# Order of two weight requests in the loop over experts: the present expert's down weights ahead of the next expert's gate and up rows

## The chip, the cores and the metric

The kernel runs on one core of one Trainium2 chip. The metric is the device time of one execution in microseconds (us). Engines are named as in the profile: PE is the matrix engine and PEld its weight loads, DVE the vector engine, ACT the scalar engine, POOL the general engine that issues gathers and scatters, and SP the engine whose instruction queue issues nearly all other DMAs (its rows are called SPq). One MB in the text is 1024 KB.

## The reference, cut to what matters

One encoder layer over 1024 tokens of width 1024: a token mixing half (projections, a convolution branch, chunked attention, merge, LayerNorm), and then a mixture of 16 experts, which is the part that the change touches.

```python
def grouped_moe(h, w_router, b_router, w_gate_up, w_down):
    ...
    combine = jnp.einsum("tk,tke->te", weights,
                         jax.nn.one_hot(sel_idx, N_EXPERTS, dtype=jnp.float32)).astype(t.dtype)
    out = jnp.zeros_like(t)
    for e in range(N_EXPERTS):
        g, u = jnp.split(t @ w_gate_up[e], 2, axis=-1)
        out = out + combine[:, e:e + 1] * ((jax.nn.silu(g) * u) @ w_down[e])
    return out.reshape(b, s, d)
```

Each token goes to two experts (TOP_K = 2), and each expert has a gate and up matrix of 1024x1024 and a down matrix of 512x1024, in float32.

## The kernel before, in words

**Tiles.** The router's result is sorted on the chip into tiles of up to 128 (token, expert) rows, each with one expert. With this input there are 21 tiles for 16 experts (`total`, line 1241): the lines of the mixture show 21 tiles, of which experts 3, 7, 8, 9 and 10 have two each and the other eleven have one. Tile 0 is expert 0's, tiles 3 and 4 are expert 3's, tile 5 expert 4's, tiles 8 to 15 are those of experts 7 to 10, tile 16 expert 11's and tile 20 expert 15's. A table `tab` says for each tile its expert (T_E), and whether the step of this tile splits the gate and up rows of the next expert (T_SPLIT_GU, set where tile i is the first of its expert) or the down rows (T_SPLIT_DN, set where tile i-1 was the first of its expert).

**Weights and their halves.** A float32 product is made of three matmuls (`mm3`, lines 1223 to 1226) of a high and a low part. So every weight row that lands is split: ACT copies the high part, DVE subtracts it and keeps the low part. For the gate and up rows these are `gu_high` (L1140) and `gu_low` (L1146), for the down rows `down_rows` on ACT (L1332) and on DVE (L1510). DVE counts `dn_lo` up by one for each of the FC = 4 down chunks that it has split.

**Buffers.** `gu` has two places, one for even and one for odd experts, each with 8 row blocks of raw (and low) and high part. `dn_raw` is single, as are `dn_h` and `dn_l`. Expert e+1's gate and up rows can land only where expert e-1's were, so `load_gu` waits for each pair of row blocks until PE has used it in the last tile of expert e-1 (`gu_rows`, L1101). Expert e's down weights can land only once `dn_raw` has been split for expert e-1 (`dn_lo`, L1121).

**Queue.** Both kinds of request are issued in order on SP in `sync_part`. Expert e+1's gate and up rows are four requests of 1 MB (L1102), expert e's down weights one request of 2 MB (L1105). Ahead of the loop SP has issued the gate and up rows of experts 0 and 1 and the down weights of expert 0. SP issues nothing else in the loop; POOL issues the gather of the tile's rows (L1161) and the scatter of its results (L1171).

**A step.** Each engine runs a step for each tile i, in its own fixed order:

- PE: transpose the gathered rows of tile i (L1248); down product of tile i-2 (`down`, 24 matmuls); transpose h of tile i-1 (L1269); gate and up product of tile i (`up`, 48 matmuls).
- ACT: high part of the transposed rows (`x_t`, L1324); if due, high parts of the down rows of tile i-1's expert (L1332), which first wait for `dn_in` and for the down product of tile i-2; high part of h of tile i-1 (L1338); if due, high parts of the next expert's gate and up rows (L1140), which wait for `gu_in` pair by pair; silu of tile i (L1348), which waits for PE's `up(i)`.
- DVE: low parts in the same order (L1504, L1510, then `y` of tile i-2, L1531, then L1514, L1146), then the product of gate and up (L1522).

So for an expert e whose first tile is i, step i splits expert e+1's gate and up rows, and step i+1 splits expert e's down rows.

Of the kernel before, what the change touches and what calls it, by code (L numbers as in the profile page):

```python
# [30 lines left out]
FC = FF // P  # L31
# [984 lines left out]
def moe(nc, sem, m):  # L1016
# [78 lines left out]
    def load_gu(sp, e, rows_before=None, pairs=range(4)):  # L1095

        for j in pairs:
            if e:
                sp.wait_ge(gu_in[j], 16 * e)
            if rows_before is not None:  # L1100
                sp.wait_ge(gu_rows, rows_before + (j + 1))  # L1101
            sp.dma_start(gu[:, place_of(e), 2 * j:2 * j + 2, 1, :].bitcast(F32), wexp[e][:, 2 * j:2 * j + 2, :]).then_inc(gu_in[j], 16)  # L1102

    def load_dn(sp, e):
        sp.dma_start(dn_raw[:], wexp[e][:, KC:WROWS, :]).then_inc(dn_in, 16)  # L1105

    def sync_part(sp):
        sp.wait_ge(x1_out, 16 * TT)
        sp.wait_ge(acc_out, 16 * TT)
        sp.wait_ge(xt_r, TT)  # L1110
        load_gu(sp, 1)
        sp.wait_ge(lg_done, TT)
        load_dn(sp, 0)
        sp.wait_ge(ids_done, 2)
        sp.wait_ge(tables, 1)
        for e in range(1, NE):
            if e + 1 < NE:

                load_gu(sp, e + 1,
                        sp.value_load(rows_i[0:1, e - 1:e], min_val=0, max_val=4 * MAX_TILES - 4))  # L1120
            sp.wait_ge(dn_lo, FC * e)  # L1121
            load_dn(sp, e)
        total = sp.value_load(cum_i[0:1, NE - 1:NE], min_val=NE, max_val=MAX_TILES)
        sp.wait_ge(gu_rows, 4 * total)
        sp.dma_start(g2_b[:], ln2_g.partition_broadcast(P)).then_inc(ln2_in, 16)
        sp.dma_start(b2_b[:], ln2_b.partition_broadcast(P)).then_inc(ln2_in, 16)
        sp.wait_ge(y_out, total * 16)
        for t in range(TT):
            sp.dma_start(xf[:, t, :], acc_dram[P * t:P * t + P, :]).then_inc(row_in[t], 16)
        for t in range(TT):  # L1130
            sp.wait_ge(f_ok, t + 1)
            sp.dma_start(out[P * t:P * t + P, :], xf[:, t, :]).then_inc(f_out, 16)
        sp.wait_ge(f_out, 16 * TT)
# [242 lines left out]
    def vector_part(dve):  # L1376
# [200 lines left out]
        for t in range(TT + 2):  # L1577
# [10 lines left out]
    return {"load_expert_0": lambda sp, j0, j1: load_gu(sp, 0, pairs=range(j0, j1)),  # L1588
            "gate_up_high_0": lambda act, k0, k1: gu_high(act, 0, place_of(0), range(k0, k1)),
            "gate_up_low_0": lambda dve, k0, k1: gu_low(dve, 0, place_of(0), range(k0, k1)), "sync": sync_part, "gpsimd": pool_part, "tensor": tensor_part,  # L1590
            "transpose_x1": transpose_x1, "logits": logits, "scalar": scalar_part, "copy_x1t": copy_x1t,
            "vector": vector_part}
# [41 lines left out]
```

## Time and profile before

| what | us |
|---|---|
| median of 3 runs | 1306.51 |
| lowest and highest run | 1303.16 and 1320.21 |
| the profiled execution's own time | 1301.75 |
| its span, first to last instruction | 1299.9 |
| PE busy (share of the span) | 1139.8 (88%) |
| DVE busy | 831.9 (64%) |
| ACT busy | 518.9 (40%) |

The mixture's tiles run from 845 to about 1250 us of the span; the loop over experts on SP issues from 854.9 to 1214.1 us. A row's start is from the start of the span. In a timeline row the first number is the start, the second the length of the merged group, and the bracket the idle time of the engine ahead of it with what ended it.

### The profile page before, as it was taken

Reading aid. Unit: us, or ns where it says so; the run is one execution under the profiler, and the core shown is the slowest. Engines: PE = TensorE matmul, PEld = TensorE weight load, DVE = VectorE, ACT = ScalarE, POOL = GpSimd, SP = SyncE. Lnnn points to the kernel's source line nnn. Section 1 sums busy time; section 2 is a strip of 40 time slices with the busy share of each in tenths; the row PEclk is TensorE's granted clock in tenths of the full one; section 3 lists DMA queues with packets and bytes.
Section 4 is the critical chain, followed back from the end, with each engine's and each line's share of the span. In section 5 each row is a group of like instructions: output and inputs, shape, how many; then the busy total and the mean of one; then the engine's idle time right before and its main releaser. Section 6 shows DMA issues by size and latency. Waiting matters only on the chain.

```text
span 1299.9 us, 17045 instructions
## 1 busy us (share of the span) xinstructions
PE 1139.8 (88%) x5600; PEld 947.6 (73%) x5601; DVE 831.9 (64%) x1128; ACT 518.9 (40%) x732; POOL 113.5 (9%) x105
## 2 busy tenths in 40 slices
PE   7999999997989999799799997289999999999720
PEld 6888888776777787677688786267888888887610
DVE  4899899215364626555476555879689655689436
ACT  5111111233375636544333212147468433467212
POOL 0000000000000000000000000002222122122118
PEclk9999999998999999899899997589999999999865
DMA  6122333320001001330513235269889876689543
GB/s 231 49 89 65 97 97 98 98 81 33 33 17 40 32 20 49 139 153 33 196 49 146 96 131 199 118 228 359 298 318 401 270 245 224 216 328 397 171 130 161
DMA packets 47701, 199.45 MB, mean 153 GB/s; under 512 B 5152, under 2 KB 5408, under 8 KB 45600
## 3 DMA queue, kind: packets, MB, share of 16 engines
q1 hardware_dynamic: 41456, 176.19, 36.1%
q0 software_dynamic: 6192, 22.55, 6.9%
q8 instruction: 34, 0.56, 0.2%
q14 instruction: 19, 0.16, 0.0%
HBM read 166.21 MB, written 32.51 MB: 153 GB/s over the span
## 4 chain that ended last, share of the span: by engine, by line
PE 73%; DVE 9%; ACT 7%; issue 5%; DMA 2%; POOL 2%; ACTq 1%; DVEq 1%; POOLq 0%; SPq 0%
PE ps L411 16%; PE ps L413 15%; PE ps L412 15%; PE ps L1224 7%; PE ps L1226 7%; PE ps L1225 7%; ACT gu L1140 2%; PE ps L1220 1%; POOL xf L1204 1%; PE ps L1248 1%; ACT pth L729 1%; DVE ptl L903 1%; DVE gu L1146 1%; PE ps L497 1%; POOL xf L1200 1%
## 5 line engine op out<-in xcount | busy, mean ns | idle before, releaser
L411 PE MATMUL ps<-xh,wh 128*128 128x512 f32 x512 | 205.9, 402 | 10.0 <-DVE xl L793 8.1
L412 PE MATMUL ps<-xl,wh 128*128 128x512 f32 x512 | 202.3, 395 | 0.0
L413 PE MATMUL ps<-xh,wl 128*128 128x512 f32 x512 | 202.1, 395 | 0.0
L816 DVE SCALAR_TENSOR_TENSOR cv<-u,dw_t,cv 128x1024 f32<-128x1024 f32 x120 | 154.1, 1284 | 3.7
L1146 DVE TENSOR_TENSOR gu<-gu (+1 forms) x128 | 147.0, 1217 | 9.1 <-ACT gu L1140 9.0
L1140 ACT ACTIVATE gu<-gu (+1 forms) x128 | 124.4, 1048 | 50.2 <-DMA gu<-in_wexp 42.4
L1224 PE MATMUL ps<-gu,xgh 128*128 x336 | 134.0, 399 | 9.0 <-DVE xgl L1504 9.0
L1226 PE MATMUL ps<-gu,xgl 128*128 x336 | 131.9, 392 | 0.0
L1225 PE MATMUL ps<-gu,xgh 128*128 x336 | 131.8, 392 | 0.0
L411 PEld LDWEIGHTS ps<-xh,wh 128*128 128x128 f32 x512 | 97.7, 191 | 33.3 <-issue 12.2
L788 DVE TENSOR_TENSOR wl<-raw,wh 128x1024 fp32r<-128x1024 f32 x52 | 63.5, 1223 | 83.8 <-ACT wh L635 83.6
L413 PEld LDWEIGHTS ps<-xh,wl 128*128 128x128 f32 x512 | 97.8, 191 | 21.2
L412 PEld LDWEIGHTS ps<-xl,wh 128*128 128x128 f32 x512 | 97.9, 191 | 20.2 <-issue 0.5
L1510 DVE TENSOR_TENSOR dn_l<-dn_raw,dn_h 128x1024 fp32r<-128x1024 f32 x64 | 74.1, 1219 | 43.3 <-ACT dn_h L1332 43.3
L1158 POOL COPY id_now<-ids_i 128x1 int32 (+1 forms) x22 | 15.0, 682 | 949.2 <-DVE to_i L1497 836.3
L635 ACT ACTIVATE wh<-raw 128x1024 fp32r<-128x1024 f32 x52 | 54.4, 1054 | 93.9 <-DMA raw<-in_wblk 93.9
L1332 ACT ACTIVATE dn_h<-dn_raw 128x1024 fp32r<-128x1024 f32 x64 | 62.4, 1047 | 73.3 <-PE ps L1226 73.3
L1224 PEld LDWEIGHTS ps<-gu,xgh 128*128 128x128 f32 x336 | 63.6, 189 | 23.5 <-issue 10.8
L1224 PE MATMUL ps<-dn_h,hbh 128*128 128x512 f32 x168 | 69.4, 413 | 12.0 <-DVE hbl L1514 7.4
L1226 PEld LDWEIGHTS ps<-gu,xgl 128*128 128x128 f32 x336 | 63.6, 189 | 13.6
L1225 PEld LDWEIGHTS ps<-gu,xgh 128*128 128x128 f32 x336 | 63.7, 190 | 12.8
L1225 PE MATMUL ps<-dn_l,hbh 128*128 128x512 f32 x168 | 67.6, 402 | 0.0
(217 smaller groups left out, 2133.9 us busy)
## 6 DMA issues: line engine op xcount, KB each, us to landing
gu<-in_wexp SPq DMA_DIRECT2D x64, 1024.0 KB
dn_raw<-in_wexp SPq DMA_DIRECT2D x16, 2048.0 KB
raw<-in_wblk SPq DMA_DIRECT2D x52, 512.0 KB, 3.6
gate_cols<-gst SPq DMA_DIRECT2D x16, 512.0 KB, 5.0
xraw<-in_xT SPq DMA_DIRECT2D x8, 512.0 KB, 7.8
gcm<-gate_cols SPq DMA_DIRECT2D x8, 512.0 KB, 7.9
gam<-gate_cols SPq DMA_DIRECT2D x8, 512.0 KB, 15.1
x<-in_x SPq DMA_DIRECT2D x8, 512.0 KB, 6.6
```

The source lines that it names most:

```text
L411: pe.matmul(o, a_h, b_h, start=first, stop=False)
L412: pe.matmul(o, a_h, b_l, start=False, stop=False)
L413: return pe.matmul(o, a_l, b_h, start=False, stop=last)
L788: dve.tensor_tensor(lo, src, hi, ALU.subtract).then_inc(w_lo, 1)
L816: dve.scalar_tensor_tensor(out=cv[:, j, :], in0=tap, scalar=w, in1=cv[:, j, :], op0=ALU.mult, op1=ALU.add).then_inc(conv_d, 1)
L1140: eng.activation(gu[:, par, k, 0, :], gu[:, par, k, 1, :].bitcast(F32), ACT.Copy).then_inc(gu_hi, 1)
L1146: eng.tensor_tensor(gu[:, par, k, 1, :], gu[:, par, k, 1, :].bitcast(F32), gu[:, par, k, 0, :], ALU.subtract).then_inc(gu_lo, 1)
L1224: pe.matmul(o, a_h, b_h, start=first, stop=False)
L1225: pe.matmul(o, a_h, b_l, start=False, stop=False)
L1226: return pe.matmul(o, a_l, b_h, start=False, stop=last)
L1332: act.activation(dn_h[:, k, :], dn_raw[:, k, :], ACT.Copy).then_inc(dn_hi, 1)
L1510: dve.tensor_tensor(dn_l[:, k, :], dn_raw[:, k, :], dn_h[:, k, :], ALU.subtract).then_inc(dn_lo, 1)
```

## The change

In the loop the wait for `dn_lo` and the request of the down weights of expert e come first, and the four requests of expert e+1 with their waits follow. The number of requests, their sizes and every wait are as before; only their order in SP's program changes.

```diff
         for e in range(1, NE):
+            sp.wait_ge(dn_lo, FC * e)
+            load_dn(sp, e)
             if e + 1 < NE:
 
                 load_gu(sp, e + 1,
                         sp.value_load(rows_i[0:1, e - 1:e], min_val=0, max_val=4 * MAX_TILES - 4))
-            sp.wait_ge(dn_lo, FC * e)
-            load_dn(sp, e)
```

## Rows read from the trace of the kernel before

**Rows 1.** The page: span, and the chain that ended last by engine

```profile
span 1299.9 us, 17045 instructions
...
PE 73%; DVE 9%; ACT 7%; issue 5%; DMA 2%; POOL 2%; ACTq 1%; DVEq 1%; POOLq 0%; SPq 0%
```

**Rows 2.** Windows: us, busy time of PE, PEld, DVE, ACT, POOL; granted clock, DMA share, GB/s

```profile
870.80:926.70 55.90, 54.78 (x260) 45.37 (x259) 50.62 (x48) 39.14 (x44) 12.73 (x11) 1.00 0.87 316
1016.60:1159.60 143.00, 143.00 (x679) 118.78 (x678) 84.46 (x81) 65.09 (x74) 26.08 (x32) 1.00 0.77 264
```

**Rows 3.** Timeline of SP's queue: requests of the expert weights

```profile
803.40 2.13 SPq L1102 DMA_DIRECT2D gu<-in_wexp  x4
...
870.83 0.34 SPq L1105 DMA_DIRECT2D dn_raw<-in_wexp  x1
871.86 6.23 SPq L1102 DMA_DIRECT2D gu<-in_wexp  x4
889.91 0.34 SPq L1105 DMA_DIRECT2D dn_raw<-in_wexp  x1
...
924.10 8.53 SPq L1102 DMA_DIRECT2D gu<-in_wexp  x4
932.68 0.49 SPq L1105 DMA_DIRECT2D dn_raw<-in_wexp  x1
941.84 8.53 SPq L1102 DMA_DIRECT2D gu<-in_wexp  x4
962.18 0.34 SPq L1105 DMA_DIRECT2D dn_raw<-in_wexp  x1
```

**Rows 4.** Timeline of DVE: the splits of the down rows (L1510)

```profile
866.18 4.62 DVE L1510 TENSOR_TENSOR dn_l<-dn_raw,dn_h 128x1024 fp32r<-128x1024 f32 x4
...
922.05 4.63 DVE L1510 TENSOR_TENSOR dn_l<-dn_raw,dn_h 128x1024 fp32r<-128x1024 f32 x4 [1.88 <-ACT dn_h L1332]
...
957.52 4.63 DVE L1510 TENSOR_TENSOR dn_l<-dn_raw,dn_h 128x1024 fp32r<-128x1024 f32 x4 [4.09 <-ACT dn_h L1332]
...
1011.96 4.63 DVE L1510 TENSOR_TENSOR dn_l<-dn_raw,dn_h 128x1024 fp32r<-128x1024 f32 x4 [0.55 <-ACT dn_h L1332]
...
1154.98 4.63 DVE L1510 TENSOR_TENSOR dn_l<-dn_raw,dn_h 128x1024 fp32r<-128x1024 f32 x4 [4.09 <-ACT dn_h L1332]
...
1209.45 4.63 DVE L1510 TENSOR_TENSOR dn_l<-dn_raw,dn_h 128x1024 fp32r<-128x1024 f32 x4 [0.50 <-ACT dn_h L1332]
```

**Rows 5.** Timeline of ACT: splits of gate and up rows, and two silus

```profile
912.65 2.01 ACT L1140 ACTIVATE gu<-gu  x2 [0.54 <-DMA gu<-in_wexp]
...
932.27 0.60 ACT L1348 ACTIVATE hb<-ps 128x512 f32<-128x512 f32 x1 [6.92 <-PE ps L1226]
...
941.27 7.70 ACT L1140 ACTIVATE gu<-gu  x8 [1.52 <-issue]
...
968.30 0.57 ACT L1348 ACTIVATE hb<-ps 128x512 f32<-128x512 f32 x1
```

**Rows 6.** Timeline of DVE: what follows a split of gate and up rows

```profile
942.52 9.17 DVE L1146 TENSOR_TENSOR gu<-gu  x8 [1.79 <-ACT gu L1140]
951.61 0.68 DVE L1522 TENSOR_TENSOR hb<-hb,ps 128x512 f32<-128x512 f32 x1
952.21 1.22 DVE L1504 TENSOR_TENSOR xgl<-ps,xgh 128x1024 fp32r<-128x1024 f32 x1
```

**Rows 7.** Windows around the burst that SP requests at 803.40 us

```profile
803.40:808.40 5.00, 3.10 (x15) 3.00 (x15) 1.32 (x5) 1.07 (x2) 0.00 (x0) 0.50 0.76 261
808.40:820.00 11.60, 1.22 (x4) 0.93 (x4) 10.57 (x32) 8.01 (x8) 0.00 (x0) 0.50 1.04 429
820.00:822.00 2.00, 0.00 (x0) 0.00 (x0) 1.93 (x3) 0.00 (x0) 0.00 (x0) 0.50 0.02 8
```

**Rows 8.** DMA queues in 860 to 1240 us: POOL's gathers and scatters

```profile
q0 software_dynamic: 5616, 20.45, 21.0%
```

**Rows 9.** Window of the down product of tile 19, after idle time of PE

```profile
1225.40:1233.10 7.70, 7.67 (x25) 6.12 (x25) 0.00 (x0) 0.00 (x0) 0.19 (x1) 0.70 0.21 83
```

**Rows 10.** The page: the group of ACT's down row splits

```profile
L1332 ACT ACTIVATE dn_h<-dn_raw 128x1024 fp32r<-128x1024 f32 x64 | 62.4, 1047 | 73.3 <-PE ps L1226 73.3
```

## The prediction

> **What bounds the kernel now.** I read the page first [rows 1]: 73% of the chain that ended last is PE, DMA 2%, so PE sets the time as a whole. But that is an average. The change lies in SP's loop, so I then read that part in windows [rows 2]. Where experts have two tiles (1016.6 to 1159.6 us) PE is busy without a gap: 143.0 us for 8 tiles, 17.9 us a tile of 72 matmuls and 12 short transposes (so some 0.23 us a matmul), with the DMA engines 77% busy. Where experts have one tile (870.8 to 926.7, four steps), they are 87% busy and PE still 98%. So PE bounds both, and DMA stands right behind it in the second kind. That is the row to worry about: every such step has to bring in 6 MB.
>
> Third view, SP's queue [rows 3], against the DVE timeline [rows 4]. It tells which wait held each request. The down request at 870.83 comes right after the down rows of expert 0 were split (866.18 + 4.62 = 870.80), the one at 889.91 likewise. There `dn_lo` is what SP waits for. At 932.68 it is not: the split had ended at 926.68, and the down request stood 6.0 us behind the four gate and up requests (924.10 to 932.63). This happens for e = 4, 8, 9, 10 and 11, where expert e-1 has two tiles. Is 6 us of use there? ACT's splits of the down rows idled 73.3 us, all of it until a PE matmul [rows 10]. None ended with the landing of the down weights. So an earlier landing buys nothing.
>
> **The change part by part.** Nothing is added or removed; five requests an expert (6 MB) swap places, and the wait for `dn_lo` now stands ahead of all five.
>
> Part 1, e = 4, 8, 9, 10, 11. The down request goes out 6 us sooner, worth 0 by the paragraph above. The first gate and up request waits for `dn_lo`: at e = 4 it goes from 924.10 to about 926.68 plus 1.0 (the distance of 870.83 to 871.86, [rows 3]), 3.6 us later; the last one stays where PE frees its rows. 2 MB are now ahead of them. From the down request to the last pair's landing I count 20.8 us (below), so 926.7 + 20.8 = 947.5. ACT starts on these rows at 941.27 and comes to the last pair 5.8 us later, at 947.0 [rows 5]. Cost 0.5 us on ACT, and DVE, which is slower (9.17 us for 8 against 7.70, [rows 5, 6]), hides it. I take 0; if that cover were gone it would be 0.5 us each, 2.5 in all.
>
> Part 2, e = 1, 2, 3, 5, 6, 7, 12, 13, 14: expert e-1 has one tile. Here lies the cost. Take e = 5. Before, expert 6's gate and up rows are requested from 941.84 on, while PE works through tile 5 [rows 3]. The wait for `dn_lo` ends only at 957.52 + 4.63 = 962.15 [rows 4], in step 6. And step 6 is the one in which ACT and DVE split expert 6's gate and up rows, whose request now starts at 963.2. They were requested 21 us ahead (first pair); now they are requested inside the step that needs them. Nothing hides that: ACT and DVE run in order, so silu and the product of this tile, the copies of the next tile's rows and the next split of down rows all stand behind L1140. And that next split is what SP waits for. It closes a ring:
>
> request → 6 MB land → last two row blocks split → next step's down split → request.
>
> Its length, term by term.
>
> - Request to last landing. The nearest row is the burst at 803.40: 4 MB and 2 MB, nothing else in flight. 261 GB/s for 5.0 us and 429 for 11.6 are 6.28e6 bytes, the whole of the 6 MB, and the engines are idle from 820.0 on [rows 7]. That is 16.7 us. POOL's gather and scatter of the step go through the same DMA engines: 21.0% of 380 us over 39 of them (20 gathers, 19 scatters) is 2.05 us each [rows 8]. The scatter is triggered by L1531, right behind the down split, and the gather by L1248, which PE reaches about 7 us after it, so both fall into the burst: 16.7 + 4.1 = 20.8 us. From below it is 16.7 (neither in it). From above it is 22.75: in the loaded trace, from the down request at 889.91 to the moment when the last pair of that round lets ACT go on, 912.65 [rows 3, 5]. I take 20.8, since in that row earlier requests were still in the queue.
> - Landing to end of the down split. ACT needs 1.0 us a block, DVE starts 1.25 us after ACT (942.52 against 941.27) and takes 1.15 a block: 3.5 us for the last pair. Then L1522 at 0.60 and L1504 at 1.15 pitch, then four blocks of L1510, 4.63 [rows 4, 6]: 9.9 us. ACT's silu (0.57, [rows 5]), its copy of the tile's rows and its own down blocks run beside this. From below 9.0, if DVE keeps up with the first block; from above 10.5.
> - SP's wake up: 870.83 - 870.80, 0.03 us; I take 0.05.
>
> One ring is 0.05 + 20.8 + 9.9 = 30.75 us. PE isn't on it: `up` and `down` are 48 and 24 matmuls, 11.0 and 5.5 us at 0.23 each, and have 30 to fit in.
>
> Nine of these replace what the trace shows from one end of a down split to another [rows 4]: 870.80 to 926.68, 962.15 to 1016.59, 1159.61 to 1214.08, together 164.8 us. Nine rings are 276.75, less 2.05 for the first (no scatter exists before tile 0 is done): 274.7. Difference +109.9 us.
>
> Part 3, leaving a ring. After each of the three runs PE sets the pace again and must first catch up. Before, `up` ended 5.6 us after the down split (932.27 against 926.68, [rows 4, 5]), 6.8 in the other two places. After, `up` starts 5.5 us after the last landing (0.2 past L1504) and needs 11.0, while the down split ends at 9.9: 6.6. Also PE has idled some 12 us in a ring, and after an idle time of 7 us the trace shows a granted clock of 0.70 over a down product, 7.70 us for what takes 5.5 at full clock [rows 9]: 2.2 more, now on the path. 8.8 less 5.6, and less 6.8 twice: 7.2 us in all. Within the rings the slower clock costs nothing, since PE has 14 us to spare there.
>
> Sum: 109.9 + 7.2 = 117 us, on the profiled execution's 1301.75 (span 1299.9): 1419. The median of the runs is 4.8 above that execution; I name 1421, a little toward it.
>
> A page of the Trainium skill speaks of one term. The trace has 6 MB at 429 GB/s in its long window [rows 7]. "DMA: Bandwidth & Descriptors", section "Where 436 GB/s comes from", says that for transfers from HBM to SBUF the HBM side, about 358 GB/s for a core, binds. By that rule the burst would take about 3 us more and nine rings 26 us more, an estimate from the page. The trace doesn't agree with the rule in its one undisturbed burst.
>
> **The rivals.**
>
> A. The transfers are slower than in the lone burst, because gather and scatter cost them more than their own 2.05 us. For it: 22.75 us in the loaded row. Against it: there the queue wasn't empty at the start. Ring 32.7, nine 294.3 (no allowance for the first), +129.5 + 7.2: 1438.
>
> By the estimate from the page, 358 GB/s would come out near A too, at 1445.
>
> B. Gather and scatter fall outside the burst, or POOL's packets cost SP's nothing. Ring 26.65, nine 239.9, +75.1 + 7.2: 1384.
>
> C. PE falls to half clock in each ring and stays there: `up` 20.6, `down` 10.3, transposes some 2 more. The down split of the next ring waits for `down` (L1332's own wait), and the ring becomes some 34.4 us: +144.8 + 16: 1462. Against it: PE would then be busy nearly all of the ring, and what the trace shows after an idle time is a return to full clock within one down product [rows 9].
>
> D. The other side: faster. Place: the requests of e = 4, 8, 9, 10, 11. If the landing of the down weights, and not PE, were the last of the two waits of L1332, five requests sent 6.0 us sooner would give back 30 us. It decides only if the later requests of Part 2 land before ACT comes to them, that is, with over 20 us of slack: 1272. Against it: the row names PE for all 73.3 us [rows 10], and ACT already waited for a gate and up pair at 912.65 with the early requests [rows 5], so there is no slack. If it gave nothing back and cost nothing, the time would stay at 1302 to 1307.
>
> **How the numbers follow.** The forecast's own case (ring 29 to 32) 0.65, A 0.15, B 0.13, C 0.04, D and no change together 0.03. The predicted time is 1421. The range takes in most of A and B: 1388 to 1446. A measurement of this kernel tells about 2% from no change (its three runs lie within 1.3% of each other); all cases but D are slower by 6% or more: faster 0.01, same 0.02, slower 0.97.
>
> **What would show it.** In the profile of the changed kernel: nine times SP issues a down request and four gate and up requests within some 4 us, right after the end of a down split, at a distance of about 31 us; ACT's L1140 waits for the DMA in nine steps, over 9 us each, where the trace of before has waits like the 0.54 at 912.65 [rows 5]; DMA share falls to some 0.65 in these stretches, and PE's clock dips in them. The stretch of experts 7 to 10 keeps 17.9 us a tile. The down splits still wait for PE or for nothing. It would be wrong if L1140's long waits were absent, if the rings were under 26 or over 33 us, or if the two-tile stretch grew.

## The result, and the profile after

The changed kernel takes 1439.4 us in the median of four runs (1436.3 to 1442.7), the kernel before 1304.8 in the same comparison: ratio 1.1005, 95% interval 1.0916 to 1.1094. The forecast was 1421 in a range of 1388 to 1446. Direction and mechanism came out as said. The size was 18 us short: it lies at the value of rival A (1438), and the range holds it because it takes in that rival.

The page of the changed kernel. DMA is now 14% of the chain that ended last, and PE 64%, where [rows 1] have 2% and 73%.

```profile
span 1437.5 us, 17045 instructions
...
PE 64%; DMA 14%; DVE 8%; issue 5%; ACT 4%; POOL 2%; SPq 1%; DVEq 1%; ACTq 0%; POOLq 0%
```

SP's queue in the changed kernel, to be read beside [rows 3].

```profile
906.62 0.34 SPq L1105 DMA_DIRECT2D dn_raw<-in_wexp  x1
907.67 2.24 SPq L1102 DMA_DIRECT2D gu<-in_wexp  x4
939.49 0.34 SPq L1105 DMA_DIRECT2D dn_raw<-in_wexp  x1
...
1146.91 0.34 SPq L1105 DMA_DIRECT2D dn_raw<-in_wexp  x1
1147.94 4.89 SPq L1102 DMA_DIRECT2D gu<-in_wexp  x4
...
1286.32 0.34 SPq L1105 DMA_DIRECT2D dn_raw<-in_wexp  x1
1287.35 2.21 SPq L1102 DMA_DIRECT2D gu<-in_wexp  x4
1318.56 0.34 SPq L1105 DMA_DIRECT2D dn_raw<-in_wexp  x1
1319.58 2.21 SPq L1102 DMA_DIRECT2D gu<-in_wexp  x4
1350.75 0.34 SPq L1105 DMA_DIRECT2D dn_raw<-in_wexp  x1
```

In the one-tile places all four gate and up requests follow the down request within 3.6 us, none of them held by PE any more, and the next group comes some 32.2 us later (1286.32, 1318.56, 1350.75; the second ring of the loop is the longest, 32.9). This is the ring of the prediction. ACT and DVE show its inside, for the ring that starts at 1318.56.

ACT:

```profile
1331.97 2.01 ACT L1140 ACTIVATE gu<-gu  x2 [15.64 <-DMA gu<-in_wexp]
1334.49 2.00 ACT L1140 ACTIVATE gu<-gu  x2 [0.51 <-DMA gu<-in_wexp]
1338.33 2.00 ACT L1140 ACTIVATE gu<-gu  x2 [1.84 <-DMA gu<-in_wexp]
1340.86 2.00 ACT L1140 ACTIVATE gu<-gu  x2 [0.52 <-DMA gu<-in_wexp]
1342.77 0.58 ACT L1348 ACTIVATE hb<-ps 128x512 f32<-128x512 f32 x1
```

DVE:

```profile
1313.90 4.62 DVE L1510 TENSOR_TENSOR dn_l<-dn_raw,dn_h 128x1024 fp32r<-128x1024 f32 x4
...
1342.09 2.36 DVE L1146 TENSOR_TENSOR gu<-gu  x2 [0.17 <-ACT gu L1140]
1344.37 0.68 DVE L1522 TENSOR_TENSOR hb<-hb,ps 128x512 f32<-128x512 f32 x1
1344.97 1.22 DVE L1504 TENSOR_TENSOR xgl<-ps,xgh 128x1024 fp32r<-128x1024 f32 x1
1346.10 4.62 DVE L1510 TENSOR_TENSOR dn_l<-dn_raw,dn_h 128x1024 fp32r<-128x1024 f32 x4
```

ACT's eight blocks were one row without a gap in [rows 5]; now they are four pairs, and ACT sits idle 15.6 us ahead of the first. "Last landing" is here the moment at which ACT, having waited for it, starts on the last pair. From the request (1318.56) to the last landing (1340.86) are 22.3 us, from there to the end of the down split (1350.72) 9.9, and SP issues 0.03 later.

The waits of the changed kernel from 860 to 1380 us (who waited, for whom, us in total, times, longest):

```profile
ACT gu L1140 <- DMA gu<-in_wexp: 177.7, 46, 16.3
DVE gu L1146 <- ACT gu L1140: 148.5, 42, 13.6
...
ACT dn_h L1332 <- PE ps L1226: 26.1, 6, 11.3
```

And its windows, with the columns of [rows 2]:

```profile
876.00:971.70 95.70, 61.57 (x250) 49.02 (x250) 51.38 (x49) 41.04 (x45) 7.33 (x11) 0.79 0.61 225
1010.80:1107.50 96.70, 57.48 (x238) 45.88 (x237) 52.56 (x49) 41.03 (x45) 8.90 (x12) 0.79 0.64 228
1254.10:1350.70 96.60, 58.88 (x242) 46.88 (x241) 52.50 (x49) 41.04 (x45) 8.92 (x12) 0.79 0.63 228
```

The three runs of one-tile experts take 95.7, 96.7 and 96.6 us, where they took 55.9, 54.4 and 54.5 [rows 4]: +124.1 of the 137.6 us by which the spans differ. No engine is busy for more than two thirds of them, DMA neither: each waits for another in turn. The stretches behind the first two of these runs grew by 3.7 and 3.6 us and the end by 1.0. The remaining 5.2 lie ahead of the loop, where the two programs are the same; an experiment with the new order below has its first down split end at 868.6 us, ahead of both, so this isn't the change's.

### The profile page after: what moved, and what is told of

It reads as the page before. It is cut to its first block, busy times and chain, and to the rows that moved or that the text cites. A ratio compares the mean times of both kernels' runs of the same rounds, so it can differ in the third digit from the quotient of the medians.

```text
span 1437.5 us, 17045 instructions
## 1 busy us (share of the span) xinstructions
PE 1171.7 (82%) x5600; PEld 968.1 (67%) x5601; DVE 835.2 (58%) x1128; ACT 520.5 (36%) x732; POOL 96.6 (7%) x105
## 3 DMA queue, kind: packets, MB, share of 16 engines
q1 hardware_dynamic: 41456, 176.19, 32.9%
## 4 chain that ended last, share of the span: by engine, by line
PE 64%; DMA 14%; DVE 8%; issue 5%; ACT 4%; POOL 2%; SPq 1%; DVEq 1%; ACTq 0%; POOLq 0%
PE ps L411 15%; PE ps L413 14%; PE ps L412 14%; DMA gu<-in_wexp 13%; PE ps L1224 6%; PE ps L1225 5%; PE ps L1226 5%; PE ps L1220 1%; POOL xf L1204 1%; DVE dn_l L1510 1%; PE ps L497 1%; ACT pth L729 1%; DVE ptl L903 1%; PE ps L1248 1%; SPq L1102 1%
## 5 line engine op out<-in xcount | busy, mean ns | idle before, releaser
L1146 DVE TENSOR_TENSOR gu<-gu (+1 forms) x128 | 150.2, 1221 | 149.2 <-ACT gu L1140 148.5
L1140 ACT ACTIVATE gu<-gu (+1 forms) x128 | 127.6, 1049 | 224.1 <-DMA gu<-in_wexp 219.5
L1224 PE MATMUL ps<-gu,xgh 128*128 x336 | 142.3, 423 | 11.2 <-DVE xgl L1504 10.1
L1225 PE MATMUL ps<-gu,xgh 128*128 x336 | 138.9, 413 | 0.0
L1226 PE MATMUL ps<-gu,xgl 128*128 x336 | 138.5, 412 | 0.0
L1269 PE MATMUL ps<-ident_t,hb 128*128 128x128 f32 x84 | 17.3, 342 | 105.4 <-DVE hb L1522 105.4
L1224 PEld LDWEIGHTS ps<-gu,xgh 128*128 128x128 f32 x336 | 68.7, 205 | 30.2 <-issue 15.9
L635 ACT ACTIVATE wh<-raw 128x1024 fp32r<-128x1024 f32 x52 | 54.4, 1054 | 94.6 <-DMA raw<-in_wblk 94.6
L1510 DVE TENSOR_TENSOR dn_l<-dn_raw,dn_h 128x1024 fp32r<-128x1024 f32 x64 | 74.0, 1220 | 23.3 <-ACT dn_h L1332 23.3
L1269 PEld LDWEIGHTS ps<-ident_t,hb 128*128 128x128 f32 x84 | 12.3, 173 | 110.9 <-DVE hb L1522 109.5
L1226 PEld LDWEIGHTS ps<-gu,xgl 128*128 128x128 f32 x336 | 67.9, 202 | 15.4
L1225 PEld LDWEIGHTS ps<-gu,xgh 128*128 128x128 f32 x336 | 68.4, 204 | 14.2
L1158 POOL COPY id_now<-ids_i 128x1 int32 (+1 forms) x22 | 5.9, 270 | 988.8 <-DVE to_i L1497 842.1
## 6 DMA issues: line engine op xcount, KB each, us to landing
gam<-gate_cols SPq DMA_DIRECT2D x8, 512.0 KB, 14.6
```

The source lines that it names most:

```text
L635: act.activation(hi, src, ACT.Copy).then_inc(w_hi, 1)
L1140: eng.activation(gu[:, par, k, 0, :], gu[:, par, k, 1, :].bitcast(F32), ACT.Copy).then_inc(gu_hi, 1)
L1146: eng.tensor_tensor(gu[:, par, k, 1, :], gu[:, par, k, 1, :].bitcast(F32), gu[:, par, k, 0, :], ALU.subtract).then_inc(gu_lo, 1)
L1224: pe.matmul(o, a_h, b_h, start=first, stop=False)
L1225: pe.matmul(o, a_h, b_l, start=False, stop=False)
L1226: return pe.matmul(o, a_l, b_h, start=False, stop=last)
```

## The experiments

Where a time comes from one run it can be off by some us: the kernel before, run 17 times beside the first experiment, took 1298.3 to 1310.4. Small differences are therefore read from distances inside the traces, and each trace is of one execution.

### Which experts carry the cost

Two kernels divide the change between the five experts whose predecessor has two tiles and the others. The first one, against the kernel before:

```diff
+            down_first = e in (4, 8, 9, 10, 11)
+            if down_first:
+                sp.wait_ge(dn_lo, FC * e)
+                load_dn(sp, e)
             if e + 1 < NE:
...
-            sp.wait_ge(dn_lo, FC * e)
-            load_dn(sp, e)
+            if not down_first:
+                sp.wait_ge(dn_lo, FC * e)
+                load_dn(sp, e)
```

> The new order only for e = 4, 8, 9, 10, 11, where expert e-1 has two tiles; the old order for the others. My theory: the down weights are never the last thing waited for there, and the gate and up rows still land in time, so the time is that of the kernel before, ratio 0.998 to 1.003 (some 1302 to 1307 us). Rival D: the 6 us by which five down requests go out sooner are of use, up to 30 us less, 1275 to 1290. Rival: the 2 MB ahead delay the gate and up rows by 2 to 4 us each in the path, 1315 to 1325, as the two longer stretches between the rings of the changed kernel could suggest.

Measured: 1308.6 us against 1305.9, ratio 1.0016, interval 0.9995 to 1.0037. No gain and no loss that can be told. In its trace the stretch of experts 7 to 10 takes 144.3 us, 1.3 more than before. That is no more than what two traces differ by where their order is the same: the first distance between two down splits is 20.6 us here and 19.1 before. Rival D is out: down requests 6 us sooner are of no use.

The second kernel has `e not in (4, 8, 9, 10, 11)`.

> The new order only for e = 1, 2, 3, 5, 6, 7, 12, 13, 14 (expert e-1 has one tile; e = 15 too, which has no gate and up request). My theory: the whole loss is here, eight rings of 32.2 us and a first of 30.6, time within 5 us of the changed kernel's 1439, 1432 to 1442. Rival: part of the loss is from the other five, then the time lies at 1420 to 1432.

Measured: 1440.9 us, one run, its rings 32.2 to 33.2 and the first 30.9. The loss is in the one-tile experts, all of it as far as one run can tell.

### The wait alone, and the ring with three quarters taken out

First the wait ahead of everything, but the gate and up requests ahead of the down request (against the kernel before):

```diff
         for e in range(1, NE):
+            sp.wait_ge(dn_lo, FC * e)
             if e + 1 < NE:
...
-            sp.wait_ge(dn_lo, FC * e)
             load_dn(sp, e)
```

> The wait for dn_lo stands first, but the gate and up requests go ahead of the down request. My theory (the wait closes the ring, the 2 MB only lengthen it): the last gate and up pair lands 5.1 us sooner, 17.2 us after the wait's end instead of 22.3, but the down weights land last and hold the next down split for some 3.5 us: ring 28 to 29 us instead of 32.2, in all 1395 to 1405. Rival (the 2 MB in front are what costs, not the wait): with the down request last, as in the kernel before, the time goes back to 1302 to 1315.

Measured: 1397.0 us, one run. Behind the first (27.1) the rings are 27.9 to 28.0 us but for two (28.9 and 28.2). The down request is back behind the gate and up requests, as in the kernel before, and two thirds of the loss remain: the wait makes the ring, the 2 MB in front only lengthen it. ACT in this kernel, one ring, for which the wait ends at 1252.55 and SP's first request goes out at 1253.21:

```profile
1258.44 2.01 ACT L1140 ACTIVATE gu<-gu  x2 [7.23 <-DMA gu<-in_wexp]
1263.11 2.01 ACT L1140 ACTIVATE gu<-gu  x2 [2.66 <-DMA gu<-in_wexp]
1266.21 2.01 ACT L1140 ACTIVATE gu<-gu  x2 [1.09 <-DMA gu<-in_wexp]
1268.76 2.00 ACT L1140 ACTIVATE gu<-gu  x2 [0.55 <-DMA gu<-in_wexp]
1274.81 3.90 ACT L1332 ACTIVATE dn_h<-dn_raw 128x1024 fp32r<-128x1024 f32 x4 [2.65 <-DMA dn_raw<-in_wexp]
```

The last pair lands 16.2 us after the wait's end instead of 22.3, and a down split (L1332) waits for the down weights themselves, 2.65 us. In no trace with the down request first does it, nor in the kernel before.

Then three of the four pairs ahead of the wait (against the kernel before):

```diff
             if e + 1 < NE:
-
-                load_gu(sp, e + 1,
-                        sp.value_load(rows_i[0:1, e - 1:e], min_val=0, max_val=4 * MAX_TILES - 4))
+                used = sp.value_load(rows_i[0:1, e - 1:e], min_val=0, max_val=4 * MAX_TILES - 4)
+                load_gu(sp, e + 1, used, pairs=range(3))
             sp.wait_ge(dn_lo, FC * e)
             load_dn(sp, e)
+            if e + 1 < NE:
+                load_gu(sp, e + 1, used, pairs=range(3, 4))
```

> Three of the four gate and up pairs are requested ahead of the wait for dn_lo and the down request, the fourth behind them. My theory: the ring stays closed by the fourth pair alone, but only 3 MB lie between the wait's end and its landing: 22.3 less 7.7 is 14.6, ring 24.5 us, nine of them +56 and leaving them +7: about 1367, between 1355 and 1375. Rival (the cost is the transfers' order in the queue, not the ring): the fourth pair comes 5.1 us later in each step, most of it hidden, 1305 to 1325.

Measured: 1356.7 us, one run, inside the range stated but 10 below the value; its rings are 20.9 to 24.0 us, not 24.5. One request of 1 MB behind the wait is enough to keep the ring. With 3, 4 and 6 MB between the wait and the last gate and up landing the rings are 20.9 to 24.0, about 28 and about 32.2 us (the middle one also holds the wait for the down weights).

### What the missing 1.5 us of a ring are

The prediction had 20.8 us from request to last landing, the trace has 22.3. Three kernels with the changed order look for the difference. The first makes every gather but tile 0's and every scatter small, 16 columns to or from fixed rows. It leaves out the sorted rows of tiles 1 to 20 and the sum over experts, so its result is not the layer's; only its times are of use:

```diff
-            pool.indirect_dma_start(out=xg[:], ...
+            if isinstance(i, int) and i == 0:
+                pool.indirect_dma_start(out=xg[:], ...
+            else:
+                pool.dma_start(xg[:, 0:16], x1_dram[0:P, 0:16]).then_inc(gath, 16)
...
-            pool.indirect_dma_start(out=acc_dram, ...
+            pool.dma_start(acc_dram[SEQ:SEQ + P, 0:16], ys[:, 0:16]).then_inc(y_out, 16)
```

> The changed kernel, but every gather after the first brings 16 columns of fixed rows instead of 1024 of the sorted ones, and every scatter writes 16 columns to the spare rows, without adding: the sorted rows of tiles 1 to 20 and the sum over experts are left out. In the changed kernel the last pair lands 22.3 us after the down request, where I had worked out 20.8 (16.7 for 6 MB alone, 4.1 for gather and scatter). Theory 1, gather and scatter cost more than their own 2.05 us each: landing at 16.7 to 17.2, rings 26.7 to 27.2. Theory 2, the missing 1.5 us lies in the start (SP's pause after the down request, the down weights in front) and has nothing to do with POOL: landing at 18.2, rings 28.1.

Measured: 1396.8 us, one run; rings of 27.9 to 28.3 us behind the first two, the length that theory 2 gave. So gather and scatter together are worth 4.1 us a ring, what the prediction had for them, and rival B (they cost the ring nothing) is out. The second keeps the gathers and makes only the scatters small; it leaves out the sum over experts:

> The changed kernel with the gathers whole and every scatter cut to 16 columns of the spare rows, without adding: the sum over experts is left out. The first ring of the changed kernel has no scatter and is 30.6 us, so all rings should come to 30.2 to 30.7 (scatter 1.5 to 2.05 us). If the scatter, which reads and writes back 512 KB, is what costs more than I took, they come to 29.4 or less.

Measured: 1412.7 us, one run; rings 29.1 to 29.6 from the third on, but for the last (28.5), and 30.7 and 30.3 ahead of them. The value of 30.2 to 30.7 fell, the other one (29.4 or less) held within 0.2 us: of the 4.1 us the scatter has 2.9 and the gather 1.2. Only the sum was right.

With POOL's traffic all but gone the last pair still lands 18.3 us after the request (1024.44 to 1042.76), not 16.7. Windows at the end of that transfer, in the kernel with small gathers and scatters (columns of [rows 2]):

```profile
1026.40:1041.00 14.60, 13.92 (x66) 11.24 (x64) 4.54 (x4) 4.86 (x5) 2.31 (x4) 1.00 0.99 401
1041.00:1041.40 0.40, 0.00 (x0) 0.00 (x0) 0.21 (x2) 0.40 (x2) 0.00 (x0) 1.00 0.72 287
1041.40:1041.80 0.40, 0.00 (x0) 0.00 (x0) 0.40 (x1) 0.40 (x1) 0.00 (x0) 1.00 0.36 143
1041.80:1042.20 0.40, 0.00 (x0) 0.00 (x0) 0.40 (x1) 0.36 (x1) 0.00 (x0) 1.00 0.11 41
1042.20:1042.80 0.60, 0.00 (x0) 0.00 (x0) 0.60 (x2) 0.04 (x1) 0.00 (x0) 0.60 0.00 0
```

Full rate ends at 1041.0, 16.6 us after the request. Then the DMA share falls for 1.2 us (0.72, 0.36, 0.11), and ACT starts 0.56 us after that. This is no property of the ring: the lone burst of [rows 7] took as long. The prediction read its engines as idle from 820.0 on, but the window 820.00:822.00 still has 8 GB/s, and a finer one shows where (kernel before):

```profile
820.00:820.40 0.40, 0.00 (x0) 0.00 (x0) 0.33 (x3) 0.00 (x0) 0.00 (x0) 0.50 0.01 0
820.55:820.60 0.05, 0.00 (x0) 0.00 (x0) 0.05 (x1) 0.00 (x0) 0.00 (x0) 0.50 0.78 328
820.60:821.20 0.60, 0.00 (x0) 0.00 (x0) 0.60 (x1) 0.00 (x0) 0.00 (x0) 0.50 0.00 0
```

The DMA columns count a packet whole in the slice in which it starts. By the trace's own record the burst's last packet, 16 KB of the down weights, starts at 820.58 and ends at 821.19, and the down request is completed at 821.65: 18.2 us after the burst's first request, where the prediction had 16.7. In the ring above, the last packet ends at 1042.20 and the last pair is completed at 1042.61, also 18.2 us after the request; ACT starts 0.15 later. So the same 6 MB take 18.2 us alone and in a ring, and with the 4.1 for gather and scatter they give 22.3, which is what was measured.

The third kernel tests another place in which time could have been missing, SP's pause of 1.0 us behind the down request (against the changed kernel):

```diff
+            if e + 1 < NE:
+                used = sp.value_load(rows_i[0:1, e - 1:e], min_val=0, max_val=4 * MAX_TILES - 4)
             sp.wait_ge(dn_lo, FC * e)
             load_dn(sp, e)
             if e + 1 < NE:
-
-                load_gu(sp, e + 1,
-                        sp.value_load(rows_i[0:1, e - 1:e], min_val=0, max_val=4 * MAX_TILES - 4))
+                load_gu(sp, e + 1, used)
```

> The changed kernel with SP's load of the row count ahead of the wait for dn_lo, so that the gate and up requests follow the down request after some 0.4 us instead of 1.0. With the gate and up requests first the 6 MB had all landed after 21.6 us instead of 22.3. If SP's pause is that 0.7 us, rings come to 31.5 to 31.6 us and the time to 5 or 6 us less. If the 2 MB cover the pause, as 5 us of transfers should, rings stay at 32.2.

Measured: SP's pause is gone (0.46 us instead of 1.03 between the two issues), the rings are 30.6, 33.0 and then 32.1 to 32.4 us, as in the changed kernel. The 2 MB cover it. (Its one run, 1433.0 us, is lower for what lies ahead of the loop: the first down split ends at 868.6 us, in the changed kernel at 876.0.)

### Whether PE is on the ring, and what covers the two-tile experts

The third of the three matmuls of the down product (the low part of h by the high part of the weights) is left out, in the changed kernel. PE then has 1.84 us less to do a tile, and the result is less exact.

```diff
-                    last = mm3(pe, ps[:, 6 + h, :], hbh[:, P * k:P * k + P], hbl[:, P * k:P * k + P],
-                               dn_h[:, k, c], dn_l[:, k, c], k == 0, k == FC - 1)
+                    pe.matmul(ps[:, 6 + h, :], hbh[:, P * k:P * k + P], dn_h[:, k, c], start=k == 0, stop=False)
+                    last = pe.matmul(ps[:, 6 + h, :], hbh[:, P * k:P * k + P], dn_l[:, k, c], start=False, stop=k == FC - 1)
```

> The changed kernel without the third of the three matmuls (low part of h by high part of the weights) in the down product: 8 matmuls, 1.84 us, fewer a tile on PE. My theory (PE isn't on the ring): rings stay at 32.2 us, the ten tiles of the two stretches where PE sets the pace lose 1.84 each, and leaving the rings and the end a little: 18 to 24 us less, 1414 to 1422. Rival C (PE, at its lower clock, sets the ring): the rings lose 1.84 to 3.7 us each as well, 1385 to 1403.

Measured: 1431.2 us, one run. The steady rings are 32.3 to 32.5 us, no shorter than with the whole product: PE isn't on them, and rival C is out. But the time missed my range. The stretch of experts 7 to 10 lost only 4.9 us (146.6 to 141.7), not 14.7: with PE faster something else is late there. So the same cut was made in the kernel before and in the kernel with the new order for e = 4, 8, 9, 10, 11 alone.

> The kernel before without the third matmul (low part of h by high part of the weights) in the down product. Where experts have two tiles PE was the bound with the old order. If it still is with 1.84 us less a tile, the stretch from tile 8's down split to tile 16's (143.0 us before) loses 14.7 and comes to 128.3, and the time to 1278 to 1290. With the changed order the same cut took only 4.9 off that stretch. If the transfers bound it there as well whatever the order, it comes to 136 to 138, and the time to 1290 to 1300.

> The new order for e = 4, 8, 9, 10, 11 only, and the down product without its third matmul. If the new order there is free only because PE covers it, the stretch of the two-tile experts comes to about 138 us, as in the changed kernel with the same cut (141.7 after a ring), some 8 to 10 us longer than with the old order. If it is free in itself, it is as long as with the old order, 128 us.

Measured: 1289.9 and 1301.9 us, one run each. From tile 8's to tile 16's down split the old order needs 131.6 us, the new order 139.8 (about 138 expected). The 131.6 is neither of the two values expected, 128.3 and 136 to 138: three of the experts lose the full 3.6 us (35.5 to 31.8), the first one only 0.6. The new order at these experts costs 8.2 us as soon as PE is a little faster. In the first experiment it cost nothing that could be told, since PE was late anyway. What is late in its place is a gate and up pair; in the changed kernel this already shows.

ACT, at expert 10's gate and up rows (down request at 1146.91):

```profile
1166.49 2.01 ACT L1140 ACTIVATE gu<-gu  x2 [0.56 <-DMA gu<-in_wexp]
1171.43 2.01 ACT L1140 ACTIVATE gu<-gu  x2 [2.93 <-DMA gu<-in_wexp]
1173.35 0.57 ACT L1348 ACTIVATE hb<-ps 128x512 f32<-128x512 f32 x1
1173.82 1.02 ACT L1324 ACTIVATE xgh<-ps 128x1024 fp32r<-128x1024 f32 x1
1176.63 3.90 ACT L1332 ACTIVATE dn_h<-dn_raw 128x1024 fp32r<-128x1024 f32 x4 [1.79 <-PE ps L1226]
```

The last pair lands 24.5 us after the down request, ACT has waited 2.93 us for it and comes to its down split with 1.79 us to spare for PE. At the down split of expert 8, one expert earlier, where no pair came late, the same wait for PE is 4.44:

```profile
1141.16 3.90 ACT L1332 ACTIVATE dn_h<-dn_raw 128x1024 fp32r<-128x1024 f32 x4 [4.44 <-PE ps L1226]
```

## Why the prediction was right, and where it was short

**Which view names the wait.** Right. The average said PE; SP's queue beside DVE's down splits said which requests would be held. The diff moves a wait of one request in front of four others, and the cost was theirs.

**Part 1, the two-tile experts, 0 us.** Right in the time (ratio 1.0016), wrong in its reason, so the 0 is partly luck. I had the last pair land 20.8 us after the down request and ACT late by 0.5, hidden by the slower DVE. In the first experiment, which has the new order at these experts alone, it lands 24.8 to 25.1 us after the request in all five, ACT waits 2.7 to 3.1 for it, and PE hides it (ACT still waits 1.3 to 2.7 us for PE at the down splits that follow, where it is 4.4 when nothing is late); in the changed kernel it is 24.5 to 24.6 and 2.9 at experts 9, 10 and 11. With PE's 1.84 us a tile gone it costs 8.2. One gather and two scatters fall into that transfer (POOL issues at 1154, 1149 and 1161 us), not one of each: 18.3 + 1.2 + 5.8 = 25.3 us by the experiments' prices, an estimate, near the 24.5. The prediction named a longer two-tile stretch as a sign against it, and that stretch did grow, by 3.6 us. 2.8 of them are in its first expert and belong to leaving the ring (part 3); 0.8 are the new order's own, between the down splits of experts 9 and 10 (36.3 us, where the kernel before and the one with the old order there have 35.5).

**Part 2, nine rings.** Right in mechanism and in how many there are: the down split's end, five requests within 3.6 us, and again. Shown by both halves of the division, by the kernel with the wait alone and by the one with three pairs ahead.

**Request to last landing, 20.8 us.** This is the step that failed: it measured 22.2 to 22.5 in seven of the eight rings behind the first, and 23.0 in the other. The 4.1 for gather and scatter held as a sum (2.9 and 1.2, not 2.05 each). The 16.7 for the burst was mis-sized by misreading [rows 7]: the engines weren't idle from 820.0 on, the last packet ended at 821.19 and the request was completed at 821.65, which makes 18.2. With POOL's traffic small a ring has the same 18.2 to completion. Nine times 1.5 is 13.5 us, most of the 14.2 by which the three stretches exceeded my 109.9. With it the ring, 32.2, came out past the 29 to 32 to which the prediction gave its best chance. Rival A had nearly the right total (ring 32.7) from a row in which ACT really waited for a pair, though not for the cause that it named, since gather and scatter cost what the prediction had for them; the row I preferred was one in which nobody waited for the last landing.

**Landing to the end of the down split, 9.9 us.** Measured 9.86. SP's wake up 0.05: 0.03.

**The first ring, 2.05 shorter.** Measured 30.6 against 32.2: 1.6. This too is near by luck: the missing scatter is worth 2.9, and something else makes the first ring longer (last section).

**Part 3, leaving the rings, 7.2 us.** Its three terms were 3.2, 2.0 and 2.0; measured are 3.7, 3.6 (2.8 without the 0.8 of part 1) and 1.0, together 8.3. `up` behind the first run of rings ends 9.1 us after the down split, where the prediction had 6.6 and 2.2 more for the clock, 8.8. But the clock's part is at another product. Windows of the changed kernel behind the first run:

```profile
966.00:971.60 5.60, 4.83 (x13) 3.69 (x14) 5.60 (x6) 3.47 (x5) 0.00 (x0) 0.50 0.00 0
971.70:980.70 9.00, 9.00 (x40) 7.37 (x40) 1.76 (x2) 0.00 (x0) 1.61 (x1) 1.00 0.90 293
```

PE has been idle for 10.3 us ahead of 966.0. The granted clock is then at its lower level (0.50, 1.2 GHz), and the first nine matmuls of `up` follow each other at 0.43 us; from 971.7 on it is at the upper level (1.00, 2.4 GHz) and they follow at 0.23. `up` takes 12.8 us, not 11.0, and the down product behind it runs at full clock. Why the end grew by 1.0 only, no experiment asks. Over the rings the granted clock is 0.79 in the mean, without effect on their length, since making PE's work shorter didn't shorten them.

**The bandwidth.** The rule of the Trainium skill that was weighed, 358 GB/s from HBM ("DMA: Bandwidth & Descriptors", "Where 436 GB/s comes from"), doesn't hold here: in the ring shown above the transfer ran at 401 GB/s over 14.6 us (DMA share 0.99), and at 375 from its first packet (1025.43) to the end of its last (1042.20). By the time alone it would have looked right, since the total (1439) fell near the 1445 to which it pointed.

## What to carry to other kernels

A wait in an in-order DMA queue holds everything behind it: before swapping two groups of requests, ask for each wait what event ends it, and whether that event itself needs what is now queued behind it. If so, the loop becomes a ring (request, transfer, split, request) in which the last transfer no longer overlaps the work that it feeds, and it gets longer though no byte was added and no engine is the bound: here from some 18 us a step to 32.

Take a transfer's landing from a consumer that waited for it, not from the end of activity in the DMA columns: here they gave 16.6 us for a transfer that was completed after 18.2, since they count a packet in the slice where it starts. Where no engine waits, the completion of the request in the trace gives it.

A reorder that measures as free is free under the present cover only: the same order at the two-tile experts cost nothing that could be told with PE as the bound, and 8.2 us with PE 1.84 us a tile faster.

## What the runs showed that was not expected

A scatter that adds 512 KB into rows in memory (L1171) makes a ring 2.9 us longer, the gather of 512 KB (L1161) 1.2 us, each by the rings of one trace against another's.

The first ring with small gathers and scatters is 29.4 us where those from the third on are 28.1, so more than the missing scatter sets its length; what, no run here tells.
